# Group norm of a recurrent layer: the heads' mean taken off where the values are turned to rows, and the group norm's products in another order

## The chip, the core and the metric

The kernel runs on one core of one Trainium2 chip. The metric is the device time of one execution in microseconds. PE is the tensor engine (its weight loads are listed apart, as PEld), DVE the vector engine, ACT the scalar engine, POOL the general engine, SP the engine that issues most DMAs. Each has its own queue of instructions, and they meet only at semaphores.

## What is computed

Two transformer blocks in float32, 512 tokens of width 1024. The second block holds an RWKV-7 time mix with 16 heads of 64 channels. The part that the change touches:

```python
o = rwkv7_recurrence(rh, decay, kh, vh, -kk, kk * ah)      # y_t = S_t r_t, S_t += v_t k_t^T, rows of S follow v
o = layer_norm(o, lnx_g.reshape(h, n), lnx_b.reshape(h, n), GN_EPS)   # mean and variance over a head's 64 channels
o = o + jnp.sum(rh * kh * r_k, axis=-1, keepdims=True) * vh           # the bonus
o = o.reshape(bsz, t, wd).astype(p.dtype) * g                         # g = sigmoid(xg) @ g_up
return o @ w_out
```

The recurrence is linear in `v`, channel by channel of a head: the output with the head's mean taken off is the output for values with the head's mean taken off.

## The kernel before

Everything is laid out with channels on the 128 partitions, as 8 blocks of 128 channels (two heads each), and time along the free axis: 528 positions (16 prefix, 512 tokens), of which the last 516 (`T3`, from `O3`) count behind the recurrence. PSUM is `acc[0]` to `acc[3]`, each with two banks; a block of 516 positions is multiplied in two halves of 258, and each half in float32 stands as two PE records. So a multiplication of one block is four PE records.

**`recurrence`** walks over five tiles of time: four of 128 positions and one of 16. In every tile `turn` brings four arrays from channels-by-time to rows-by-channels with `nc.tensor.transpose`, four blocks at a time (`g` is 0 or 1): `TM_V` is the values `v` (the trace's `rw_v`), `TM_A` is `kk` (its `x2r`), `TM_B` and `TM_K` are `a` and `k` (its `rw_a` and `rw_k`). The order on PE is written by hand: `rows_of_v(ti, 0)`, `rows_of_a(ti)`, `rows_of_v(ti, 1)`, then `tail(ti)`, whose first products (`z`, line 2664) need the turned values. ACT copies those from PSUM into `uv` (line 2757), DVE copies part of the others. SP and POOL send small DMAs that invert the diagonal blocks (`at_spill`, `dia`, `inverse`, `MD`, `MTD`).

**`group_norm_and_gate`** is a program block of its own between two barriers, with four hand-written queues. First loop, for each block `i`: PE multiplies `o` by `mean64` (a mean over each head) into `acc[i % 2]`; DVE subtracts it from `o` in place (line 3141); ACT squares the result (line 3114); PE sums squares into 16 rows, one for each head (`of_heads`, line 3064 into `acc[2]`). Beside it DVE makes the product `r * r_k * k` (line 3130), PE sums it over heads by `ones64` into `acc[3]`, and DVE multiplies `v` by it (line 3147). The trace's names: `gn_scratch` is squares and products, `rw_a` is `o`. Then ACT takes the square root over 16 rows (line 3116), DVE the reciprocal (line 3149).

Second loop, for each block `i`: PE spreads the 16 rows to 128 channels (`gn_root` by `gn_own`) into `acc[i % 2]`, DVE multiplies `o` by it (line 3152), ACT applies gain and offset (line 3122), POOL adds the weighted `v` (line 3166), PE makes the gate (`xg` by two slabs of `g_up`, eight records) into `acc[2 + i % 2]`, and DVE multiplies (line 3136). POOL and ACT also split the first two weight slabs of the next stage (`mg_whi`, `mg_wlo`). The next stage, `merge`, begins behind a barrier.

Of the kernel before, what the change touches and what calls it, by code (L numbers as in the profile page):

```python
# [263 lines left out]
def program(nc, x_t, slabs, moe_slabs, params_d, router_bias, const0, const1, const2, meta_rows, final_row, out):  # L264
    top = ExitStack()
    with top:
# [40 lines left out]
        def k0(name, n=P, at=0):  # L307
            return c0[:, C0[name] + at:C0[name] + at + n]
# [2001 lines left out]
        def recurrence(r, k, v, kk, a, o, wc, k2, kk_r, last_y):  # L2310
# [129 lines left out]
            with ExitStack() as nx, block() as b:  # L2440
# [22 lines left out]
                dia, inv = sbt(nx, "dia", [P, 272]), sbt(nx, "inv", [P, 272])  # L2463

# [20 lines left out]
                def _(pe):  # L2485
# [129 lines left out]
                    def turn(ti, w, g, out_bank):  # L2615
                        t0, n = tiles[ti][0:2]
                        for q in range(4):
                            first, count = (t0 + CH, P if stays(ti + 1) else CH) if w == TM_B else (t0, n)
                            mm = nc.tensor.transpose(bank(out_bank)[0:count, q * P:(q + 1) * P],
                                                     arrays[w][:, 4 * g + q, first:first + count], k0("ident"))  # L2620
                        did(mm, "pe", ti, "tm", w, g)
# [21 lines left out]
                    def rows_of_v(ti, g):  # L2643
                        if ti == 0:
                            pe.wait_ge(v_back[0], 16)
                            after(pe, "act", 0, "at", 1)
# [175 lines left out]
                def _(dve):  # L2822
# [84 lines left out]

                    step(nc.vector.memset(S[0][:, :, :], 0.0))
# [133 lines left out]
        def group_norm_and_gate(xt, r, k, v, o, xg, k2, h, w):  # L3042
# [3 lines left out]
            meaned, centred, squared, varred, rooted = (sem("gn_" + n) for n in ("meaned", "centred", "squared", "varred", "rooted"))  # L3046
# [3 lines left out]
            with ExitStack() as nx, block() as b:  # L3050
                view = lambda i: xt[:, 2 * i:2 * i + 2, :].rearrange("p a t -> p (a t)")[:, 0:T3]
                sq, prod = [view(0), view(1)], [view(2), view(3)]
# [5 lines left out]
                owned = sem("gn_owned")  # L3058

                @b.tensor  # L3060
                def _(pe):
                    def over(j, mat, x, rows=P, start=True, stop=True):
                        for s, (lo, hi) in enumerate(halves(T3)):
                            mm = nc.tensor.matmul(acc[j][0:rows, s, 0:hi - lo], mat, x[:, lo:hi], start=start, stop=stop)
                        return mm

                    def variance(i):
                        pe.wait_ge(squared, i + 1)
                        over(2, of_heads(i), sq[i % 2], 16, i == 0, i == 7).then_inc(varred, 1)
# [12 lines left out]
                    n = SLAB0["g_up"]  # L3082
                    pe.wait_ge(sig, 1)
                    slab_wait(pe, n)
                    slab_wait(pe, n + 1)
                    pe.wait_ge(centred, 8)
                    pe.wait_ge(bonus_read, 8)
                    pe.wait_ge(inverted, 1)
                    pe.wait_ge(owned, 1)

                    def gate(i):
                        if i >= 2:
                            pe.wait_ge(gated, i - 1)
                        for q in range(2):
                            mm = over(2 + i % 2, ring[(n + q) % RING][:, i * P:(i + 1) * P], xg[:, q, O3:], P, q == 0, q == 1)
                        mm.then_inc(g_ready, 1)

                    for i in range(8):
# [9 lines left out]
                def _(act):  # L3108
                    nc.scalar.activation(xg[:, :, :], xg[:, :, :], ACT.Sigmoid).then_inc(sig, 1)
                    for i in range(8):  # L3110
# [15 lines left out]
                def _(dve):  # L3126
                    tt = nc.vector.tensor_tensor

                    def product(i):
                        nc.vector.scalar_tensor_tensor(out=prod[i % 2], in0=r[:, i, O3:], scalar=pcol("r_k", i), in1=k[:, i, O3:],  # L3130
                                                       op0=ALU.mult, op1=ALU.mult).then_inc(prod_made, 1)
# [6 lines left out]
                    product(0)  # L3138
                    for i in range(8):
                        dve.wait_ge(meaned, i + 1)  # L3140
                        tt(fold(o[:, i, O3:], T3), fold(o[:, i, O3:], T3), A(i % 2, T3), ALU.subtract).then_inc(centred, 1)
                        if i + 1 < 8:
                            if i >= 1:
                                dve.wait_ge(bonus, i)
                            product(i + 1)
                        dve.wait_ge(bonus, i + 1)
                        tt(fold(v[:, i, O3:], T3), fold(v[:, i, O3:], T3), A(3, T3), ALU.mult).then_inc(bonus_read, 1)
# [11 lines left out]
                def _(pool):  # L3159
                    nc.gpsimd.tensor_copy(own[:, :, :], k0("ident")[0:16, 0:16].unsqueeze(2).to_broadcast([16, 16, 64])).then_inc(owned, 1)  # L3160
                    w.pool(pool, w.ahead("gate_b")[0])
                    for i in range(8):
                        if i == 4:
                            w.pool(pool, w.ahead("gate_b")[1])
# [244 lines left out]
```

## Time and profile before

| | us |
|---|---|
| median of 3 runs | 2117.97 |
| the runs | 2116.71, 2117.97, 2130.38 |
| the profiled execution's own time | 2116.82 |
| its span in the trace | 2115.0 |
| PE busy in the span | 1941.1 (92%) |
| DVE busy | 1305.3 (62%) |
| recurrence, in the trace | about 1280 to 1476 |
| group norm and gate | about 1476 to 1534 |

The profiled execution's time is 1.8 us more than its span, which counts from the first to the last instruction. Its time is 1.15 us under the median. Durations below come from this one execution. In the rows a start and a duration in us stand first; `x4` says that four records were merged; the bracket at the end gives how long the engine had been idle and what ended that.

### The profile page before, as it was taken

How to read it: one execution, taken by the hardware profiler on the slowest of the kernel's cores; microseconds unless marked ns; L12 is line 12 of the kernel's file. 1: busy time of each engine (PE TensorE's matmuls, PEld its weight loads, DVE VectorE, ACT ScalarE, POOL GpSimd, SP SyncE). 2: the span in 40 equal slices, each digit the busy share in tenths (PEclk: the TensorE clock that was granted, in tenths of full speed). 3: DMA queues.
4: the chain of work that ended last, by engine and by line, in shares of the span. 5: the costliest groups of instructions: out<-in, count | busy, mean ns of one | idle time of the engine just before them, and what ended most of it. 6: DMA issues, size and time to landing. Idle time of an engine off the chain costs nothing. (4 is left out here: it accounts for less than half of the span.)

```text
span 2115.0 us, 36683 instructions
## 1 busy us (share of the span) xinstructions
PE 1941.1 (92%) x14678; PEld 1652.9 (78%) x14678; DVE 1305.3 (62%) x2000; ACT 906.9 (43%) x1381; POOL 691.9 (33%) x370
## 2 busy tenths in 40 slices
PE   7999999997999996799999996888999989999997
PEld 4786836764778775799999775787599989999784
DVE  2678758334798997589973674664522178878302
ACT  4314238434788877522233651333242243333312
POOL 2433300330121212243445213320236235555441
PEclk9999999999999998899999898998999999999999
DMA  5222210123999997223223114210042122222221
GB/s 184 90 80 80 80 60 2 61 80 135 401 362 385 360 378 303 70 98 114 91 86 125 61 45 114 36 27 29 20 161 90 51 80 93 90 98 90 78 92 40
DMA packets 91313, 260.08 MB, mean 123 GB/s; under 512 B 26320, under 2 KB 29536, under 8 KB 90528
## 3 DMA queue, kind: packets, MB, share of 16 engines
q1 hardware_dynamic: 87424, 247.90, 32.8%
q0 software_dynamic: 3744, 10.11, 1.4%
q8 instruction: 107, 1.75, 0.3%
q14 instruction: 38, 0.31, 0.0%
HBM read 239.10 MB, written 18.87 MB: 122 GB/s over the span
## 5 line engine op out<-in xcount | busy, mean ns | idle before, releaser
L1578 DVE TENSOR_TENSOR moe_wlo<-moe_ring,moe_whi 128x1024 fp32r<-128x1024 f32 x198 | 233.2, 1224 | 38.8 <-ACT moe_whi L1574 37.8
L547 PE MATMUL acc<-h_xhi,h_whi 128*128 128x264 f32 x816 | 233.5, 286 | 7.0 <-DVE h_xlo L461 3.7
L547 PE MATMUL acc<-h_xlo,h_whi 128*128 128x264 f32 x816 | 233.9, 287 | 0.0
L547 PE MATMUL acc<-h_xhi,h_wlo 128*128 128x264 f32 x816 | 233.5, 286 | 0.0
L1574 ACT ACTIVATE moe_whi<-moe_ring 128x1024 fp32r<-128x1024 f32 x198 | 205.9, 1058 | 40.2 <-PE acc L1635 21.5
L400 POOL TENSOR_TENSOR h_wlo<-ring,h_whi 128x1024 fp32r<-128x1024 f32 x59 | 141.6, 2401 | 249.0 <-ACT h_whi L391 248.8
L547 PE MATMUL acc<-ff_xhi,ff_whi 128*128 128x258 f32 x704 | 200.8, 285 | 9.4 <-DVE ff_xlo L461 9.4
L547 PE MATMUL acc<-ff_xhi,ff_wlo 128*128 128x258 f32 x704 | 199.7, 284 | 0.0
L547 PE MATMUL acc<-ff_xlo,ff_whi 128*128 128x258 f32 x704 | 199.7, 284 | 0.0
L547 PEld LDWEIGHTS acc<-h_xhi,h_whi 128*128 128x128 f32 x816 | 155.8, 191 | 8.6 <-DVE h_xlo L461 4.1
L2141 DVE SCALAR_TENSOR_TENSOR acc<-cp,par,acc 128x528 f32<-128x528 f32 x232 | 159.4, 769 | 0.0
L547 PEld LDWEIGHTS acc<-h_xlo,h_whi 128*128 128x128 f32 x816 | 155.6, 191 | 0.0
L547 PEld LDWEIGHTS acc<-h_xhi,h_wlo 128*128 128x128 f32 x816 | 154.9, 190 | 0.0
L400 POOL TENSOR_TENSOR in_wlo<-ring,in_whi 128x1024 fp32r<-128x1024 f32 x39 | 95.7, 2456 | 156.0 <-ACT in_whi L391 156.0
L400 POOL TENSOR_TENSOR ff_wlo<-ring,ff_whi 128x1024 fp32r<-128x1024 f32 x44 | 115.4, 2626 | 90.4 <-ACT ff_whi L391 90.4
L547 PEld LDWEIGHTS acc<-ff_xhi,ff_whi 128*128 128x128 f32 x704 | 134.1, 190 | 10.9 <-issue 8.3
L547 PEld LDWEIGHTS acc<-ff_xlo,ff_whi 128*128 128x128 f32 x704 | 134.3, 191 | 0.0
L547 PEld LDWEIGHTS acc<-ff_xhi,ff_wlo 128*128 128x128 f32 x704 | 133.8, 190 | 0.0
L547 PE MATMUL acc<-in_xhi,in_whi 128*128 128x512 f32 (+1 forms) x280 | 114.5, 409 | 7.3 <-DVE in_xlo L461 7.3
L3341 DVE SCALAR_TENSOR_TENSOR ff_t<-ff_up,par,ff_t 128x516 f32<-128x516 f32 x44 | 116.2, 2641 | 1.6
L547 PE MATMUL acc<-in_xlo,in_whi 128*128 128x512 f32 (+1 forms) x280 | 111.6, 399 | 0.0
L547 PE MATMUL acc<-in_xhi,in_wlo 128*128 128x512 f32 (+1 forms) x280 | 111.5, 398 | 0.0
(502 smaller groups left out, 4993.9 us busy)
## 6 DMA issues: line engine op xcount, KB each, us to landing
ring<-slabs SPq DMA_DIRECT2D x213, 512.0 KB, 3.5
moe_ring<-moe_slabs SPq DMA_DIRECT2D x204, 512.0 KB, 6.3
tok_rows<-h_tok SPq DMA_DIRECT2D x5, 512.0 KB, 4.0
h_spill<-x2r SPq DMA_DIRECT2D x1, 2112.0 KB, 9.2
v_spill<-rw_v SPq DMA_DIRECT2D x1, 2112.0 KB, 7.4
y_spill<-cp SPq DMA_DIRECT2D x8, 264.0 KB, 4.7
x2r<-h_spill SPq DMA_DIRECT2D x1, 2112.0 KB
x2r<-y_spill SPq DMA_DIRECT2D x1, 2112.0 KB, 10.1
```

Source lines behind the costliest of these rows:

```text
L400: nc.gpsimd.tensor_tensor(self.lo[at][:, :], ring[n % RING][:, :], self.hi[at][:, :].bitcast(F32), ALU.subtract).then_inc(lo_made, 1)
L547: mm = nc.tensor.matmul(acc[j][0:rows, s, 0:t1 - t0], wp[:, at:at + rows], xp[:, t0:t1], start=(k == 0 and m == 0), stop=(k == kt - 1 and ...
L1574: nc.scalar.activation(whi[u % AHEAD][:, :], ringm[u % RAW][:, :], ACT.Copy).then_inc(w_hi, 1)
L1578: tensor_tensor(wlo[u % AHEAD][:, :], ringm[u % RAW][:, :], whi[u % AHEAD][:, :].bitcast(F32), ALU.subtract).then_inc(w_lo[u % 2], 1)
L2141: ins = nc.vector.scalar_tensor_tensor(out=d, in0=x, scalar=tap(q, j), in1=csum(q), op0=ALU.mult, op1=ALU.add)
L3341: nc.vector.scalar_tensor_tensor(out=d, in0=up[i % 4][:, 2:2 + T3], scalar=tap(2), in1=d, op0=ALU.mult, op1=ALU.add).then_inc(tapped, 1)
```

## The change

The recurrence gets a matrix `less_mean` = identity minus the heads' mean (one DVE operation ahead of its first instructions), and `turn` multiplies the values by it instead of transposing them: 40 `transpose` calls become 40 `matmul` calls of the same 128x128 shape (five tiles, two groups, four blocks). The array `v` itself stays, so the bonus still sees the full values. PE waits for the matrix once.

In `group_norm_and_gate` the mean products and DVE's eight subtractions are gone. The products for the bonus are made in place in `r`, so that they need no buffers, and there are four buffers for squares in place of two. ACT squares first and takes the sigmoid after. The bonus products use `acc[0]`, `acc[1]`, `acc[3]` in turn. The first gate stands ahead of the last five bonuses, and in the loop gate `i` now follows spread `i`; before, gate `i - 1` followed it.

```diff
+                less_mean, less_made = sbt(nx, "less_mean", [P, P]), sem("rec_less_mean")
...
-                            mm = nc.tensor.transpose(bank(out_bank)[0:count, q * P:(q + 1) * P],
-                                                     arrays[w][:, 4 * g + q, first:first + count], k0("ident"))
+                            rows, x = bank(out_bank)[0:count, q * P:(q + 1) * P], arrays[w][:, 4 * g + q, first:first + count]
+                            if w == TM_V:
+                                mm = mmul(rows, x, less_mean[:, :], start=True, stop=True)
+                            else:
+                                mm = nc.tensor.transpose(rows, x, k0("ident"))
...
+                    tt(less_mean[:, :], k0("ident"), k0("mean64"), ALU.subtract).then_inc(less_made, 1)
...
PE of group_norm_and_gate:
-                    for i in range(8):
-                        if i >= 2:
-                            pe.wait_ge(centred, i - 1)
-                        over(i % 2, k0("mean64"), o[:, i, O3:]).then_inc(meaned, 1)
-                        pe.wait_ge(prod_made, i + 1)
-                        if i >= 1:
-                            pe.wait_ge(bonus_read, i)
-                        over(3, k0("ones64"), prod[i % 2]).then_inc(bonus, 1)
-                        if i >= 1:
-                            variance(i - 1)
-                    variance(7)
+                    for i in range(8):
+                        pe.wait_ge(squared, i + 1)
+                        over(2, of_heads(i), sq[i % 4], 16, i == 0, i == 7).then_inc(varred, 1)
...
+                    def bonuses(which):
+                        for i in which:
+                            pe.wait_ge(prod_made, i + 1)
+                            if i >= 3:
+                                pe.wait_ge(bonus_read, i - 2)
+                            over(bonus_at(i), k0("ones64"), prod(i)).then_inc(bonus, 1)
...
                     def gate(i):
                         if i >= 2:
                             pe.wait_ge(gated, i - 1)
...
+                    bonuses(range(3))
+                    pe.wait_ge(sig, 1)
...
+                    pe.wait_ge(rooted, 1)
+                    gate(0)
+                    bonuses(range(3, 8))
+                    pe.wait_ge(inverted, 1)
...
                     for i in range(8):
-                        if i >= 2:
+                        if i < 2:
+                            pe.wait_ge(bonus_read, 7 + i)
+                        else:
                             pe.wait_ge(scaled, i - 1)
                         over(i % 2, to_channels(i), root).then_inc(spread, 1)
                         if i >= 1:
-                            gate(i - 1)
-                    gate(7)
+                            gate(i)
ACT:
-                    nc.scalar.activation(xg[:, :, :], xg[:, :, :], ACT.Sigmoid).then_inc(sig, 1)
                     for i in range(8):
-                        act.wait_ge(centred, i + 1)
-                        if i >= 2:
-                            act.wait_ge(varred, i - 1)
-                        nc.scalar.activation(sq[i % 2], o[:, i, O3:], ACT.Square).then_inc(squared, 1)
+                        if i >= 4:
+                            act.wait_ge(varred, i - 3)
+                        nc.scalar.activation(sq[i % 4], o[:, i, O3:], ACT.Square).then_inc(squared, 1)
+                    nc.scalar.activation(xg[:, :, :], xg[:, :, :], ACT.Sigmoid).then_inc(sig, 1)
DVE:
-                    product(0)
                     for i in range(8):
-                        dve.wait_ge(meaned, i + 1)
-                        tt(fold(o[:, i, O3:], T3), fold(o[:, i, O3:], T3), A(i % 2, T3), ALU.subtract).then_inc(centred, 1)
...
+                        nc.vector.scalar_tensor_tensor(out=prod(i), in0=r[:, i, O3:], scalar=pcol("r_k", i), in1=k[:, i, O3:],
+                                                       op0=ALU.mult, op1=ALU.mult).then_inc(prod_made, 1)
+                    weigh(0)
                     dve.wait_ge(rooted, 1)
                     nc.vector.reciprocal(root[:, :], root[:, :]).then_inc(inverted, 1)
+                    for i in range(1, 8):
+                        weigh(i)
```

DVE's second loop is the same as before: for block `i` it multiplies by the spread root, then does the gate product of block `i - 2`. POOL splits both slabs before its additions, and waits in each for `bonus_read` too.

How the instructions stand, first on PE where the second loop begins; `gn_root,gn_own` is a spread, `xg,ring` a gate. Before:

```order
L3064 MATMUL acc2<-gn_scratch,c2 16x258 x4
L3064 MATMUL acc0<-gn_root,gn_own 128x258 x2
L3064 MATMUL acc1<-gn_root,gn_own 128x258 x2
L3064 MATMUL acc2<-xg,ring1 128x258 x2
L3064 MATMUL acc2<-xg,ring2 128x258 x2
L3064 MATMUL acc0<-gn_root,gn_own 128x258 x2
L3064 MATMUL acc3<-xg,ring1 128x258 x2
L3064 MATMUL acc3<-xg,ring2 128x258 x2
L3064 MATMUL acc1<-gn_root,gn_own 128x258 x2
L3064 MATMUL acc2<-xg,ring1 128x258 x2
```

After (bonus products are `x2r,c0`):

```order
L3071 MATMUL acc0<-x2r,c0 128x258 x2
L3071 MATMUL acc1<-x2r,c0 128x258 x2
L3071 MATMUL acc0<-gn_root,gn_own 128x258 x2
L3071 MATMUL acc1<-gn_root,gn_own 128x258 x2
L3071 MATMUL acc3<-xg,ring1 128x258 x2
L3071 MATMUL acc3<-xg,ring2 128x258 x2
L3071 MATMUL acc0<-gn_root,gn_own 128x258 x2
L3071 MATMUL acc2<-xg,ring1 128x258 x2
L3071 MATMUL acc2<-xg,ring2 128x258 x2
L3071 MATMUL acc1<-gn_root,gn_own 128x258 x2
```

The third spread (block 2) was followed by the gate of block 1 in `acc3`; now it is followed by the gate of block 2 in `acc2`, which holds the gate of block 0 until DVE has read it.

On DVE, the start of the group norm (`rw_v,acc` is the bonus put on the values). Before:

```order
L3130 SCALAR_TENSOR_TENSOR gn_scratch<-x2r,par,rw_k 128x516
L3141 TENSOR_TENSOR rw_a<-rw_a,acc0 128x516
L3130 SCALAR_TENSOR_TENSOR gn_scratch<-x2r,par,rw_k 128x516
L3147 TENSOR_TENSOR rw_v<-rw_v,acc3 128x516
L3141 TENSOR_TENSOR rw_a<-rw_a,acc1 128x516
L3130 SCALAR_TENSOR_TENSOR gn_scratch<-x2r,par,rw_k 128x516
```

After:

```order
L3144 SCALAR_TENSOR_TENSOR x2r<-x2r,par,rw_k 128x516 x8
L3136 TENSOR_TENSOR rw_v<-rw_v,acc0 128x516
L3148 RECIPROCAL gn_root<-gn_root 16x516
L3136 TENSOR_TENSOR rw_v<-rw_v,acc1 128x516
L3136 TENSOR_TENSOR rw_v<-rw_v,acc3 128x516
```

All eight products stand first and the subtractions are gone; one bonus multiplication stands ahead of the reciprocal, seven behind it, where all eight were ahead.

## Rows read from the trace of the kernel before

**Rows 1.** Windows of PE: stretch, length, busy, granted clock, DMA share, GB/s.

```profile
1476.00:1502.00 26.00, 25.10 (x96) 0.92 0.22 84
1502.00:1534.50 32.50, 27.70 (x96) 0.84 0.00 1
```

**Rows 2.** Timeline, first vector operation of the group norm, one turn of its first loop.

```profile
1476.47 1.55 DVE L3130 SCALAR_TENSOR_TENSOR gn_scratch<-x2r,par,rw_k 128x516 f32<-128x516 f32 x1 [4.47 <-PEq L2440]
...
1494.79 1.14 PE L3064 MATMUL acc<-rw_a,c 128*128 128x258 f32 x4
...
1495.77 2.01 PE L3064 MATMUL acc<-gn_scratch,c 128*128 128x258 f32 x8
...
1496.69 0.63 ACT L3114 ACTIVATE gn_scratch<-rw_a 128x516 f32<-128x516 f32 x1 [2.28 <-DVE rw_a L3141]
...
1497.71 1.14 PE L3064 MATMUL acc<-rw_a,c 128*128 128x258 f32 x4
```

**Rows 3.** Timeline, from that loop to the spread and gate loop.

```profile
1500.26 1.28 ACT L3116 ACT_TABLE_LOAD   x1
1501.61 0.68 ACT L3116 ACTIVATE gn_root<-acc,c 16x516 f32<-16x516 f32 x1
...
1502.32 3.37 DVE L3149 RECIPROCAL gn_root<-gn_root 16x516 f32<-16x516 f32 x1 [1.87 <-ACT gn_root L3116]
...
1505.93 3.78 PE L3064 MATMUL acc<-gn_root,gn_own 16*128 16x258 f32 x8 [4.37 <-DVE gn_root L3149]
```

**Rows 4.** Timeline, one turn of the spread and gate loop, and its end.

```profile
1519.79 1.14 PE L3064 MATMUL acc<-gn_root,gn_own 16*128 16x258 f32 x4
...
1520.86 2.01 PE L3064 MATMUL acc<-xg,ring 128*128 128x258 f32 x8
1520.97 0.69 DVE L3152 TENSOR_TENSOR rw_a<-rw_a,acc 128x516 f32<-128x516 f32 x1 [1.71 <-PE acc L3064]
1521.58 0.69 DVE L3136 TENSOR_TENSOR rw_a<-rw_a,acc 128x516 f32<-128x516 f32 x1
...
1522.80 1.14 PE L3064 MATMUL acc<-gn_root,gn_own 16*128 16x258 f32 x4
...
1533.74 0.69 DVE L3136 TENSOR_TENSOR rw_a<-rw_a,acc 128x516 f32<-128x516 f32 x1 [1.05 <-PE acc L3064]
...
1536.52 0.36 PE L547 MATMUL acc<-mg_xhi,mg_whi 128*128 128x258 f32 x1 [2.89 <-DVE mg_xlo L461]
```

**Rows 5.** Timeline, the turned values in the fourth of five tiles.

```profile
1435.08 0.66 PE L2619 MATMUL acc<-c,rw_v 128*128 128x128 f32 x4
...
1435.57 1.04 PE L2619 MATMUL acc<-c,x2r 128*128 128x128 f32 x8
1435.77 2.50 ACT L2757 ACTIVATE uv<-acc 64x512 f32<-64x512 f32 x4
...
1436.45 0.60 PE L2619 MATMUL acc<-c,rw_v 128*128 128x128 f32 x4
...
1438.33 1.01 PEld L2664 LDWEIGHTS acc<-uv,M 64*64 64x64 f32 x32 [0.25 <-ACT uv L2757]
```

**Rows 6.** Source line 2702: eight multiplications by the identity.

```profile
L2702 PE MATMUL acc<-c,rw_a x16: 272/272/294, 1280.1 to 1281.7; 128*64 128x128 f32 x16
```

**Rows 7.** Timeline of PE, the wait in the first tile.

```profile
1309.19 3.04 PE L2528 MATMUL acc<-MD,ot 64*64 64x64 f32 x52 [12.64 <-DMA MD<-inverse]
```

**Rows 8.** Windows of PE, as rows 1, for the granted clock.

```profile
1189.50:1204.00 14.50, 14.50 (x52) 0.53 0.16 58
...
1464.00:1466.00 2.00, 2.00 (x22) 0.50 0.00 0
...
1480.00:1482.00 2.00, 1.99 (x9) 0.98 0.97 414
...
1514.00:1516.00 2.00, 2.00 (x9) 0.94 0.00 0
```

**Rows 9.** Groups by line and form, 1180 to 1205.

```profile
L1957 PE MATMUL acc<-late,kk_own 16*128 16x264 f32 x8 | 3.3, 545 | 0.0
```

More of the change, by code:

```diff
@@ L2645, in rows_of_v @@
                             pe.wait_ge(v_back[0], 16)
+                            pe.wait_ge(less_made, 1)
                             after(pe, "act", 0, "at", 1)
@@ L3042, in group_norm_and_gate @@
         def group_norm_and_gate(xt, r, k, v, o, xg, k2, h, w):
-            meaned, centred, squared, varred, rooted = (sem("gn_" + n) for n in ("meaned", "centred", "squared", "varred", "rooted"))
+            squared, varred, rooted = (sem("gn_" + n) for n in ("squared", "varred", "rooted"))
             inverted, spread, scaled, shifted = (sem("gn_" + n) for n in ("inverted", "spread", "scaled", "shifted"))
@@ L3050, in group_norm_and_gate @@
             with ExitStack() as nx, block() as b:
-                view = lambda i: xt[:, 2 * i:2 * i + 2, :].rearrange("p a t -> p (a t)")[:, 0:T3]
-                sq, prod = [view(0), view(1)], [view(2), view(3)]
+                sq = [xt[:, 2 * i:2 * i + 2, :].rearrange("p a t -> p (a t)")[:, 0:T3] for i in range(4)]
+                prod = lambda i: r[:, i, O3:]
                 root = sbt(nx, "gn_root", [16, T3])
@@ L3058, in group_norm_and_gate @@
                 owned = sem("gn_owned")
+                bonus_at = lambda i: (0, 1, 3)[i % 3]
                 @b.tensor
@@ L3096, in gate @@
                         mm.then_inc(g_ready, 1)
+                    bonuses(range(3))
+                    pe.wait_ge(sig, 1)
+                    slab_wait(pe, n)
+                    slab_wait(pe, n + 1)
+                    pe.wait_ge(rooted, 1)
+                    gate(0)
+                    bonuses(range(3, 8))
+                    pe.wait_ge(inverted, 1)
+                    pe.wait_ge(owned, 1)
                     for i in range(8):
-                        if i >= 2:
+                        if i < 2:
+                            pe.wait_ge(bonus_read, 7 + i)
+                        else:
                             pe.wait_ge(scaled, i - 1)
@@ L3108, in _ @@
                 def _(act):
+                    for i in range(8):
+                        if i >= 4:
+                            act.wait_ge(varred, i - 3)
+                        nc.scalar.activation(sq[i % 4], o[:, i, O3:], ACT.Square).then_inc(squared, 1)
                     nc.scalar.activation(xg[:, :, :], xg[:, :, :], ACT.Sigmoid).then_inc(sig, 1)
-                    for i in range(8):
-                        act.wait_ge(centred, i + 1)
-                        if i >= 2:
-                            act.wait_ge(varred, i - 1)
-                        nc.scalar.activation(sq[i % 2], o[:, i, O3:], ACT.Square).then_inc(squared, 1)
                     act.wait_ge(varred, 8)
@@ L3127, in _, with weigh @@
                     tt = nc.vector.tensor_tensor
-                    def product(i):
-                        nc.vector.scalar_tensor_tensor(out=prod[i % 2], in0=r[:, i, O3:], scalar=pcol("r_k", i), in1=k[:, i, O3:],
-                                                       op0=ALU.mult, op1=ALU.mult).then_inc(prod_made, 1)
+                    def weigh(i):
+                        dve.wait_ge(bonus, i + 1)
+                        tt(fold(v[:, i, O3:], T3), fold(v[:, i, O3:], T3), A(bonus_at(i), T3), ALU.mult).then_inc(bonus_read, 1)
                     def gate(i):
@@ L3136, in gate @@
                         tt(fold(o[:, i, O3:], T3), fold(o[:, i, O3:], T3), A(2 + i % 2, T3), ALU.mult).then_inc(gated, 1)
-                    product(0)
                     for i in range(8):
-                        dve.wait_ge(meaned, i + 1)
-                        tt(fold(o[:, i, O3:], T3), fold(o[:, i, O3:], T3), A(i % 2, T3), ALU.subtract).then_inc(centred, 1)
[L3142 to L3147, printed above, removed]
+                        nc.vector.scalar_tensor_tensor(out=prod(i), in0=r[:, i, O3:], scalar=pcol("r_k", i), in1=k[:, i, O3:],
+                                                       op0=ALU.mult, op1=ALU.mult).then_inc(prod_made, 1)
+                    weigh(0)
                     dve.wait_ge(rooted, 1)
                     nc.vector.reciprocal(root[:, :], root[:, :]).then_inc(inverted, 1)
+                    for i in range(1, 8):
+                        weigh(i)
                     for i in range(8):
@@ L3160, in _ @@
                     nc.gpsimd.tensor_copy(own[:, :, :], k0("ident")[0:16, 0:16].unsqueeze(2).to_broadcast([16, 16, 64])).then_inc(owned, 1)
-                    w.pool(pool, w.ahead("gate_b")[0])
+                    for n in w.ahead("gate_b"):
+                        w.pool(pool, n)
                     for i in range(8):
-                        if i == 4:
-                            w.pool(pool, w.ahead("gate_b")[1])
+                        pool.wait_ge(bonus_read, i + 1)
                         pool.wait_ge(shifted, i + 1)
```

9 lines of the change are left out of this document (removed).

## The prediction

> **What bounds the kernel now.** The chain that ended last is of no use here: it reaches back only to the last barrier, far behind this change. So I read the two places one by one in the timeline, each for the wait that ends last, and the granted clock of the tensor engine beside them. In the group norm PE is busy for 25.1 of 26 us in the first loop and 27.7 of 32.5 us in the second [rows 1]. One turn of the first loop lasts from 1494.79 to 1497.71, 2.92 us, for twelve PE records (mean, bonus, variance), while DVE, ACT and POOL have idle time [rows 2]: at full clock a record costs some 0.22 us, and PE is the bound. Between the loops PE stands still for 4.37 us, for the root (0.68) and the reciprocal (3.37) [rows 3]. In the second loop a turn lasts 3.01 us, again twelve records; a spread alone holds PE for 1.07 us (1519.79 to 1520.86), a gate for 1.94 [rows 4]. Both loops so follow PE. The stage lasts from 1476.47 to the end of the last gate product at 1533.74 + 0.69 = 1534.43 [rows 2, 4], 58.0 us. In the recurrence the turned values stand in a chain too: PE turns, ACT copies, and the second half of the `z` products starts when ACT is through [rows 5].
>
> The clock matters at both ends. It is low (0.50 of full, 1.2 of 2.4 GHz) in 1464 to 1466 though PE is busy all of it, at 0.98 in 1480 to 1482, and 0.94 in 1514 to 1516 [rows 8]. From 0.92 over 26 us it was low for 0.08 x 26 x 2 = 4.2 us in the first loop, and from 0.84 over 32.5 us for 10.4 us around the wait for the reciprocal [rows 1].
>
> **The change part by part.** **Turned values.** A transpose is one PE record; in rows 5 eight take 0.88 us (1435.57 to 1436.45), 0.11 each. A float32 multiplication is two records: line 2702, with the same 128 moving columns and weights of 64, has 16 for eight calls, in (1281.7 - 1280.1) / 15 = 0.107 us each [rows 6]. So four calls cost 0.44 us more, and a tile has two groups of four. ACT's copies of the first group start 0.44 later. Those of the second wait for PE: its eight records start 0.44 later than 1436.45 and take 0.88 plus some 0.16 of tail, so ACT starts at 1437.95 and is done two copies (half of 2.50) later, at 1439.2, where `z` now goes on at 1438.33 [rows 5]. That is 0.9 us a tile. Behind it PE has no free time until the next tile's first products, so nothing absorbs it, in four of the five tiles: 3.6 us. In the first tile PE waits 12.64 us for a DMA of the inverse [rows 7], which starts from other data; there it is hidden. Bounds: 0, if other slack takes all, and 4.5 with the first tile. The matrix itself is one DVE operation of 128 elements, ahead of work that DVE waits for anyway: 0 to 0.5 us, taken as 0.
>
> **First part of the group norm.** Gone are 32 mean records and eight subtractions. Squares need nothing now: the first takes 0.63 us [rows 2], and PE starts 0.9 us into the stage. It then has eight variances of four records. At full clock one is 0.87 us; at the low clock 1.72. If the clock rises 3.6 us into the stage, as now, 1.6 variances are done by then and 6.4 x 0.87 = 5.6 follow: 9.2 us. The other rise of this stage came 8.3 us after PE went to work again (1505.93 to 1514.2, from the 0.94) [rows 3, 8]; with that 4.3 variances are low and it is 11.5. I take 10.3. ACT is hidden: eight squares, a table load of 1.28 us [rows 3], a sigmoid over twice the width, so some 1.1 (an estimate), and another load of 1.28 come to 8.7 us, or some 10.2 with the waits for buffers, and the root (0.68) waits for the last variance.
>
> From the end of the variances on: three bonus products on PE, 2.6 us, then the gate of block 0, 1.94. Meanwhile DVE puts the first bonus on the values and starts the reciprocal about 1.8 us behind the variances, done 5.2 us behind them. So 3.37 us of reciprocal now lie beside 4.5 us of PE work, and the 4.37 us gap goes. What is late next is the pair of PE and DVE in bonuses 3 to 7: bonus 4 needs the values of block 1 weighed, and from there each is 0.87 us; the last is weighed 10.4 us behind the variances, and spread 1 starts at 10.5. Spread 0 lies ahead of it. Then 1.07 + 1.94 for spread 1 and gate 1: spread 2 starts at 10.3 + 10.5 + 3.0 = 23.8 us.
>
> **Second loop.** Here the order costs. Gate `i` waits until DVE has read gate `i - 2` from the same bank, and DVE does that behind its product with spread `i`. Before, gate `i - 1` stood there, whose bank was free long ago. A turn is now: spread start to DVE's product 1.18 us (1519.79 to 1520.97), to DVE's gate product 0.61, that product 0.69, some 0.15 back to PE, gate 1.94 [rows 4]: 4.57 us in place of 3.01. Queued behind PE's wait is the next spread, and DVE waits for that. Five turns bring spread 7 to 23.8 + 22.8 = 46.6. Then 2.6 to the start of gate 7, 2.05 until DVE can read it, 0.69: 51.9 us. ACT and POOL, which kept pace with the turn of 3.01, stay hidden in the longer turn. The next stage is reached the same 2.1 us behind DVE's last product as now [rows 4]; its first slabs are freed by the same gate.
>
> **The sum**: 51.9 against 58.0 is 6.1 us less, with ends 7.2 and 4.9 by the clock; with 3.6 more in the recurrence, 2.5 us less. On the profiled execution's 2116.8 that is 2114.3, on the median of 2118.0 it is **2115.5**.
>
> A rule for the turned values: rows 5 and 6 say that a multiplication costs two transposes. The Trainium skill (TensorE: Matmul & The Clock Gate, Terms) says that transpose mode is four times faster for float32. By it a group of four would cost 1.32 us more and not 0.44; it is rival 3 below.
>
> **The rivals.** **1, slower: variances of 16 columns don't raise the clock.** They are 16 columns wide and now stand alone, where they were mixed with full ones. For: in 1464 to 1466 PE is busy all the time with narrow products, at 0.50; from 1189.5 to 1204 it is busy without a gap for 14.5 us at 0.53, in a stage where products of 16 rows, 545 ns each, stand among full ones [rows 8, 9]. Against: those had few rows, these have 128. Then all eight variances take 1.72 us, 13.8 + 0.9 = 14.7, 4.4 more than summed, and the bonuses and the first gate begin low as well, 4.0 more: 8.4 - 2.5 = 5.9 slower, 2123.9. It decides against the change as soon as the clock rises over 2.5 us later than I took.
>
> **2, the clock falls in the second loop.** PE would idle 1.5 of 4.57 us there. For: it fell in the 4.37 us gap before. Against: the gaps are a third of that. Each low turn costs 12 x 0.215 = 2.6 us. A stretch of some 8 us, as now behind the gap, costs 3: 2118.5. The whole loop costs 17: 2132.6.
>
> **3, multiplications at four times a transpose**: 0.88 more a group, eight groups, 7.0 more: 2122.5. Against it stands rows 6, the same form of product.
>
> **4, the second loop doesn't stall**, because the bank is free in time: 6 x 1.56 = 9.4 less, 2106.1. Against it: the order of both queues.
>
> **5, the clock holds in the last tile.** PE ran low from 1464 at the latest until 1480 [rows 8], 12 us of it in the recurrence; if that were at full clock and three quarters of it busy (an estimate), 4.5 less: 2111.0. The Trainium skill (the same page, Part 4: PE-mode transpose) says that transposes don't count as a busy engine. No row here separates that.
>
> **How the numbers follow.** A measurement of this kernel can tell about 1%, 21 us. Chances: my sum 0.50 (its own range 2112 to 2118), rival 1 0.20, rival 2 0.12 for one stretch and 0.04 for the loop, rival 3 0.03, rival 4 0.05, rival 5 0.04, others 0.02. The range reaches from 2109 to 2126: it takes in the sum, rivals 1, 3, 5 and the short form of 2, and leaves out the whole loop, rival 4 and the rest. All of these lie within 1%: 0.97, with 0.01 for faster and 0.02 for slower.
>
> **What the profile would show.** Right: 80 records of `less_mean` with `rw_v`, eight per group 0.107 apart; the tile's `z` 0.9 us later behind its turn; the stage 51 to 53 us; no gap of over 1.5 us on PE around the reciprocal; a turn of 4.5 us in the second loop with PE idle for 1.5 ahead of each gate. Wrong: a granted clock at 0.50 past 8 us of the stage (rival 1) or in the second loop (rival 2); a turn of 3.0 (rival 4). What would upset the sum from outside is a shift of the DMAs of the inverse in the recurrence, which have about 4 us of slack behind PE in the middle tiles.

## The result and the profile after

The changed kernel takes 2130.11 us (median of 20 runs, 2120.04 to 2135.77), the kernel before 2119.45 (20 runs, 2111.84 to 2131.08). The ratio is 1.0039, with a 95% interval of 1.0026 to 1.0053: some 8 us slower (the two medians lie 10.7 apart). That is within 1%, as forecast, but above the range, and on the other side of no change from the 2.5 us less that the sum gave. The profiled execution took 2120.04 us (span 2118.3), the shortest of its 20, so a second one was profiled later (experiment 10).

**The group norm after**, in the timeline: start, duration, work, and in the bracket the idle time before it.

```profile
1478.58 2.20 ACT L3118 ACTIVATE gn_scratch<-rw_a 128x516 f32<-128x516 f32 x4 [0.34 <-PEq L2440]
...
1479.26 9.00 PE L3071 MATMUL acc<-gn_scratch,c 128*16 128x258 f32 x32 [1.35 <-ACT gn_scratch L3118]
...
1489.98 3.36 DVE L3148 RECIPROCAL gn_root<-gn_root 16x516 f32<-16x516 f32 x1
...
1494.04 3.73 PE L3071 MATMUL acc<-x2r,c 128*128 128x258 f32 x16 [0.34 <-DVE rw_v L3136]
...
1501.62 1.13 PE L3071 MATMUL acc<-gn_root,gn_own 16*128 16x258 f32 x4
1504.14 2.01 PE L3071 MATMUL acc<-xg,ring 128*128 128x258 f32 x8 [1.39 <-DVE rw_a L3141]
1506.08 1.14 PE L3071 MATMUL acc<-gn_root,gn_own 16*128 16x258 f32 x4
1508.60 2.01 PE L3071 MATMUL acc<-xg,ring 128*128 128x258 f32 x8 [1.39 <-DVE rw_a L3141]
1510.54 1.14 PE L3071 MATMUL acc<-gn_root,gn_own 16*128 16x258 f32 x4
1513.06 3.14 PE L3071 MATMUL acc<-xg,ring 128*128 128x258 f32 x8 [1.39 <-DVE rw_a L3141]
1516.13 2.08 PE L3071 MATMUL acc<-gn_root,gn_own 16*128 16x258 f32 x4
1519.60 3.81 PE L3071 MATMUL acc<-xg,ring 128*128 128x258 f32 x8 [1.39 <-DVE rw_a L3141]
...
1528.73 2.08 PE L3071 MATMUL acc<-gn_root,gn_own 16*128 16x258 f32 x4
...
1538.89 0.55 PE L547 MATMUL acc<-mg_xhi,mg_whi 128*128 128x258 f32 x1 [2.89 <-DVE mg_xlo L461]
```

Read it against [rows 2 to 4]. The first part is as meant: eight variances in one run of 32 records, done 9.7 us into the stage (1479.26 + 9.00 - 1478.58); the reciprocal lies beside bonuses and a gate, and PE's longest gap there is 0.34 us where it was 4.37. The spread of block 2 starts at 1501.62, 23.0 us into the stage. Then every gate has 1.39 us of idle PE ahead of it, released by DVE's gate product. At first a turn takes 4.46 us. But the same four spread records that last 1.14 us at 1510.54 last 2.08 at 1516.13, and the same eight gate records go from 2.01 to 3.81. The gap has not grown; PE itself has become slow.

**Granted clock**, in windows of PE: stretch, length, busy, granted clock, DMA share, GB/s.

```profile
1478.57:1537.37 58.80, 48.08 (x160) 0.79 0.10 38
1478.57:1503.40 24.83, 23.14 (x92) 0.91 0.23 88
...
1503.40:1513.50 10.10, 6.59 (x26) 1.00 0.00 0
1513.50:1524.00 10.50, 9.12 (x22) 0.51 0.00 0
1524.00:1527.00 3.00, 1.61 (x8) 1.00 0.00 0
1527.00:1537.37 10.37, 7.62 (x18) 0.52 0.03 5
1538.80:1544.80 6.00, 5.91 (x28) 0.52 0.99 376
```

The second loop falls from full clock (1.00, 2.4 GHz) to the lower level (0.51, 1.2 GHz), comes back for 3 us, falls again, and hands the low clock on to the next stage. There, in the kernel before, the clock was up:

```profile
1536.50:1542.50 6.00, 5.98 (x50) 1.00 1.04 414
```

Fifty records there, 28 here in as many microseconds: 22 x 0.12 = 2.6 us lost behind the stage as well. Not all of it comes from the loop: in experiments 1, 2, 3 and 5 to 8, whose loops end at full clock, the same 6 us hold some 37 records, at 0.72. So 9 records, 1.1 us, go with the low clock that the loop hands on. The other 13, 1.6 us, are lost in those seven as well but not in experiment 9, and no run shows why. The whole stage, from the first DMA of the group norm to the first of the next stage, is 58.80 us, and in the kernel before it was 58.57 (1476.43 to 1535.00). In between lies a row of before, the spread of block 2:

```profile
1513.38 1.54 PE L3064 MATMUL acc<-gn_root,gn_own 16*128 16x258 f32 x4
```

It stood 36.9 us into the stage there and stands 23.0 us into it now, 13.9 earlier. From it to the end of DVE's last gate product it was 21.1 us (to 1534.43), and is 35.2 (to 1536.11 + 0.69 = 1536.80), 14.1 more. What the first part gives, the second takes.

**The recurrence after**: the line of the new product, then the fourth tile in PE's timeline, to be held against [rows 5].

```profile
L2622 PE MATMUL acc<-less_mean,rw_v x80: 272/275/583, 1287.5 to 1464.4; 128*128 128x128 f32 x64, 128*16 128x128 f32 x16
```

```profile
1437.14 1.16 PE L2622 MATMUL acc<-less_mean,rw_v 128*128 128x128 f32 x8
1438.13 1.04 PE L2624 MATMUL acc<-c,x2r 128*128 128x128 f32 x8
...
1439.99 1.15 PE L2669 MATMUL acc<-uv,M 64*64 64x64 f32 x32
1441.34 1.15 PE L2669 MATMUL acc<-uv,M 64*64 64x64 f32 x32 [0.20 <-ACT uv L2762]
```

A group of four is eight records and takes 0.99 us (1437.14 to 1438.13), before 0.49. The second half of `z` starts 4.20 us behind the turn, before 3.25 (1435.08 to 1438.33): 0.95 a tile. From the first DMA of the inverse to the group norm it is 176.91 us against 174.74.

### The profile page after: what moved, and what is told of

Same layout as the page of the kernel before. It is cut to its first block and busy times, and to the rows that moved or that the text cites. A ratio compares the mean times of both kernels' runs of the same rounds, so it can differ in the third digit from the quotient of the medians.

```text
span 2118.3 us, 36694 instructions
## 1 busy us (share of the span) xinstructions
PE 1943.8 (92%) x14686; PEld 1656.1 (78%) x14686; DVE 1299.8 (61%) x1993; ACT 906.6 (43%) x1381; POOL 690.6 (33%) x370
## 5 line engine op out<-in xcount | busy, mean ns | idle before, releaser
L547 PEld LDWEIGHTS acc<-ff_xhi,ff_whi 128*128 128x128 f32 x704 | 133.7, 190 | 11.7 <-issue 8.3
```

Source lines behind the costliest of these rows:

```text
L547: mm = nc.tensor.matmul(acc[j][0:rows, s, 0:t1 - t0], wp[:, at:at + rows], xp[:, t0:t1], start=(k == 0 and m == 0), stop=(k == kt - 1 and ...
```

## The experiments

Each ran against the kernel before on the same chip. The ratios have 95% intervals. "Recurrence" below is the stretch from its first `inverse<-inv` DMA to the first DMA of the group norm, "stage" the stretch from there to the first DMA of the next stage, both from the one profiled execution.

**1. The turned values alone**, in the kernel before.

```diff
+                            if w == TM_V:
+                                mm = mmul(rows, x, less_mean[:, :], start=True, stop=True)
+                            else:
+                                mm = nc.tensor.transpose(rows, x, k0("ident"))
```

> The kernel before, with one part of the change alone: the values are turned by the multiplication with less_mean; the group norm is as before, mean products and subtractions too. Theory A (the stall for the gate's bank and the clock it costs explain the slowdown; the turned values cost PE records and no more): the group norm starts 2 to 3.6 us later than before's and lasts 58 us; in all 2 to 4 us slower, ratio 1.001 to 1.002. Theory B (the multiplications disturb the recurrence, by the clock or by the inverse's DMAs, and explain the slowdown): 8 us or more slower, ratio 1.004 or more.

Measured: 2128.44 us, ratio 1.0033 (1.0012 to 1.0055). In its profile the windows of PE give

```profile
1300.69:1482.45 181.76, 148.44 (x3872) 0.88 0.15 27
1482.45:1540.72 58.27, 52.49 (x192) 0.88 0.11 39
```

The stage is that of before, the recurrence 7 us longer. Its fourth tile reads as in the changed kernel (`z` 4.21 us behind the turn), so the records explain four times 0.95 us. The rest goes with the granted clock, 0.88 over this stretch where it was 0.90, and is seen in places: the 26 us from 1344 to 1370 ran at 1.00 in the kernel before and at 0.87 here and in the changed kernel, while 1396 to 1404 went from 0.79 to 1.00. The turned values alone are a loss. Their 1.0033 lies between the two expectations, and its interval holds both: it allows the 3.6 us summed, and it allows all of the changed kernel's loss. It takes the next experiment to tell the theories apart.

**2. The gate one block behind the spread again**, all else as changed.

```diff
                         over(i % 2, to_channels(i), root).then_inc(spread, 1)
-                        if i >= 1:
-                            gate(i)
+                        if i >= 2:
+                            gate(i - 1)
+                    gate(7)
```

> The changed kernel with one order undone: in the second loop gate i-1 follows spread i again, for i from 2, and gate 7 comes last; gate 0 stays early. Theory A: a turn falls from 4.46 to 3.0 us, PE idles under 0.5 us in it, the clock stays at full, and the stage lasts 58.2 - 5 x 1.45 - 5 or so for the clock = 46 to 49 us; in all 8 to 14 us faster than the changed kernel, so 0.995 to 0.999 of before. Theory B: the stage gets shorter, but the total stays within 3 us of the changed kernel's, since the loss sits in the recurrence. Theory C (the clock falls in this loop whatever the order, from 16-row products): the turn is 3.0 us at full clock but low-clock turns of over 5 us stay.

Measured: 2109.93 us, 0.9942 (0.9921 to 0.9963). Timeline of PE in the second loop:

```profile
1503.68 3.08 PE L3071 MATMUL acc<-gn_root,gn_own 16*128 16x258 f32 x12
1506.69 3.60 PE L3071 MATMUL acc<-xg,ring 128*128 128x258 f32 x8
1510.22 1.14 PE L3071 MATMUL acc<-gn_root,gn_own 16*128 16x258 f32 x4
1511.29 2.01 PE L3071 MATMUL acc<-xg,ring 128*128 128x258 f32 x8
1513.23 1.14 PE L3071 MATMUL acc<-gn_root,gn_own 16*128 16x258 f32 x4
```

```profile
1484.02:1528.44 44.42, 42.01 (x160) 0.90 0.14 51
1506.70:1509.90 3.20, 3.20 (x9) 0.50 0.01 3
```

No bracket, so no idle time, and turns of 3.01 us as in [rows 4]. The gain is more than was expected (46 to 49 us of stage, a ratio of 0.995 at best): moving one call takes 14.4 us off the stage and turns a loss of 0.4% into a gain of 0.6%. The order of the second loop is the cause; whether by the wait itself or by the clock that follows from it is the next question.

One thing here is not explained by waits. The clock is low for 3.2 us from 1506.70 on, with PE busy all the time and 0.34 us its only gap since the variances began. In this order three spreads stand in a row ahead of that stretch, twelve records of 16 rows. Experiments 5, 7 and 8 have the same loop, and each has its low stretch at that place (9.7 us long in experiment 5); experiment 6, with two spreads in a row and a single gap of 0.19 us, has none. That the narrow products bring it fits, but no run here varies them alone.

**3. The changed kernel with PE kept busy in the wait**: three products by the identity into columns of the other product's bank that nobody uses.

```diff
                         if i >= 2:
+                            for f in range(3 if i < 7 else 0):
+                                nc.tensor.matmul(acc[3 - i % 2][:, f % 2, 258:512], k0("ident"), xg[:, 0, O3:O3 + 254], start=True, stop=True)
                             pe.wait_ge(gated, i - 1)
```

> The changed kernel with work added in the wait: ahead of PE's wait for the gate's bank, in turns 2 to 6 of the second loop, three useless 128x128 products over 254 columns (six records, 1.3 us at full clock) go to unused columns of a bank that nobody reads then. The stall of 1.39 us stays in time but PE is busy in it. Theory A split in two: if the clock falls because PE idles, the granted clock stays at 1.00 to the end of the loop, the turn stays at 4.5 us, and the stage lasts 51 to 53 us in place of 58.2, 5 to 8 us faster than the changed kernel. If the clock falls for another reason, low turns get longer than 7.2 us and the kernel is slower than the changed one.

Measured: 2123.13 us, 0.9997 (0.9979 to 1.0015).

```profile
1516.17 1.14 PE L3071 MATMUL acc<-gn_root,gn_own 16*128 16x258 f32 x4
1517.24 1.55 PE L3090 MATMUL acc<-xg,c 128*128 128x254 f32 x6
1518.69 2.01 PE L3071 MATMUL acc<-xg,ring 128*128 128x258 f32 x8
1520.63 1.14 PE L3071 MATMUL acc<-gn_root,gn_own 16*128 16x258 f32 x4
```

```profile
1492.33:1544.39 52.06, 48.27 (x190) 0.94 0.12 44
1545.90:1551.90 6.00, 5.99 (x37) 0.72 1.01 370
```

All turns take 4.46 us, and none is low, though the gap ahead of gate 7 is left open. The wait is as long as before; only PE is busy in five of its six turns. The order and the spreads are the same, so in this loop it is the gaps that bring the clock down. That the spreads' 16 rows have no part in it isn't shown: the filling products have 128 rows, and experiment 2 had a low stretch without a gap. This is the kernel that the prediction described: its last gate product ends 51.5 us into the stage (DVE's line at 1543.12 and its 0.69), beside the 51.9 of the sum. Against experiment 2 it prices the wait at 7.6 us of stage (11.7 by the ratios, but each has an interval of some 4 us to either side), and against the changed kernel the clock at 6.7 us of stage in this profile, and 1.0039 - 0.9997 = 0.42%, 9 us, in the times.

**4. The kernel before with the gate at once**, nothing else changed.

```diff
                         over(i % 2, to_channels(i), root).then_inc(spread, 1)
-                        if i >= 1:
-                            gate(i - 1)
-                    gate(7)
+                        gate(i)
```

> The kernel before, with the gate's place alone changed: gate i follows spread i for all i, and waits for gate i-2 to be read. Everything else is as before. Theory A: turns of 4.46 us and more from turn 2 on, PE idle 1.39 us in each, clock down in part of the loop; the stage lasts 64 to 72 us, 6 to 14 us slower than before, ratio 1.003 to 1.007. Theory B: within 3 us of before.

Measured: 2139.46 us, 1.0095 (1.0065 to 1.0125), the slowest of all, and slower than was expected (6 to 14 us more, a stage of 64 to 72).

```profile
1520.94 2.08 PE L3064 MATMUL acc<-gn_root,gn_own 16*128 16x258 f32 x4
1524.41 3.81 PE L3064 MATMUL acc<-xg,ring 128*128 128x258 f32 x8 [1.39 <-DVE rw_a L3134]
1528.14 2.08 PE L3064 MATMUL acc<-gn_root,gn_own 16*128 16x258 f32 x4
```

```profile
1477.49:1556.59 79.10, 65.02 (x192) 0.72 0.08 28
```

The same gap of 1.39 us, and turns of 7.20 us: here the clock has just come back from the gap for the reciprocal (a turn of 3.01 us, from 1512.77), and it falls in the first turn that has a gap. The stage grows by 20.5 us and the time by 0.95%, 20 us. Of the 4.2 us more per turn the wait is 1.45 (4.46 less 3.01) and the clock 2.74 (7.20 less 4.46).

**5. Experiment 2 with the values turned by a transpose.**

```diff
-                            if w == TM_V:
+                            if False:
                                 mm = mmul(rows, x, less_mean[:, :], start=True, stop=True)
```

> The kernel with gate i-1 behind spread i (the second experiment's), with the values turned by plain transposes again. It leaves out that the heads' mean is taken off, so its output is that without the mean removed; every other instruction stays. Theory A (a multiplication costs its extra PE records, 0.9 us a tile on the path, and at times a stretch of low clock): 4 to 7 us faster than the second experiment's kernel, 0.991 of before; from the first inverse's DMA to the start of the group norm 175 to 177 us in place of 183. Theory D (the turn is hidden, and the first experiment's 0.33% had another reason): the same time as the second experiment's kernel within 2 us.

This kernel leaves out that the heads' mean is taken off, so it is a yardstick and no choice.

Measured: 2104.42 us, 0.9922 (0.9893 to 0.9951), with a profiled execution of 2122.24, the slowest of its six. Beside experiment 2 (0.9942) it is 0.20%, 4 us, less, but the intervals overlap. The profiles agree better: the recurrence with transposes took 174.74, 177.09, 174.75 and 177.51 us (before, experiments 4, 9 and this one), mean 176.0; turned by the matrix in the changed order, 176.91, 181.76, 183.14, 182.14, 179.72 and 181.22 (changed, 1, 2, 3, 6, 10), mean 180.8. That is 4.8 us for five tiles, with one profile of each kernel and a spread of 6 us among the second six.

**6. DVE's gate product first**: in the changed kernel DVE does the gate of block `i - 2` before it waits for spread `i`.

```diff
                     for i in range(8):
-                        dve.wait_ge(spread, i + 1)
-                        tt(fold(o[:, i, O3:], T3), fold(o[:, i, O3:], T3), A(i % 2, T3), ALU.mult).then_inc(scaled, 1)
                         if i >= 2:
                             gate(i - 2)
+                        dve.wait_ge(spread, i + 1)
+                        tt(fold(o[:, i, O3:], T3), fold(o[:, i, O3:], T3), A(i % 2, T3), ALU.mult).then_inc(scaled, 1)
```

> The changed kernel with PE's order left as changed and DVE's order altered: in turn i of the second loop DVE does the gate product of block i-2 ahead of its product with spread i. If the slowdown is PE's wait for the bank that DVE reads too late (theory A), the wait goes: a turn is 3.0 us, PE idles under 0.5 us, the clock stays up, and the stage lasts about 44 us as in the second experiment, 0.994 of before. If it is that the gate of the same block stands directly behind its spread on PE, whatever DVE does (rival), turns stay at 4.4 us and more and the total stays near the changed kernel's.

Measured: 2109.7 us, 0.9956 (0.994 to 0.9972).

```profile
1508.50 1.14 PE L3071 MATMUL acc<-gn_root,gn_own 16*128 16x258 f32 x4
...
1509.57 2.01 PE L3071 MATMUL acc<-xg,ring 128*128 128x258 f32 x8
```

PE keeps the changed order and hardly waits (0.19 us once, ahead of gate 2): the spread at 1508.50 and the next at 1511.51 are 3.01 us apart, the granted clock is 1.00 through the loop, and the stage is 44.03 us. So the loss lies in the pair of orders, and either side mends it.

**7. Both groups of values turned first**, with the loop of experiment 2: in each tile, so that ACT's copies of the second group don't follow the turn of `kk`.

```diff
                             rows_of_v(ti, 0)
-                            rows_of_a(ti)
                             rows_of_v(ti, 1)
+                            rows_of_a(ti)
```

> The second experiment's kernel, with the turn of the values ahead in each tile: both groups of values, then kk, where kk stood between the two groups. If what is on the path is ACT's copies behind PE's second group (theory A), the z products' second half goes on 3.3 to 3.8 us behind the turn's start in place of 4.2, and the kernel is 1 to 3 us faster than the second experiment's. If PE's records alone are the path (rival), the total is the same within 1 us, since as many records stand there.

Measured: 2107.38 us, 0.9936 (0.9917 to 0.9956).

```profile
1438.71 2.05 PE L2622 MATMUL acc<-less_mean,rw_v 128*128 128x128 f32 x16
...
1441.57 2.08 PE L2669 MATMUL acc<-uv,M 64*64 64x64 f32 x64
```

`z` now runs in one piece and its second half starts about 3.9 us behind the turn (1438.71 to 1441.57 and half of 2.08), 0.3 less, where 0.4 to 0.9 less was expected. The recurrence is 179.81 us. Its gain over experiment 2 can't be told from none, so which of the two theories holds stays open. It has the lowest ratio of the kernels here that compute everything: 0.6% faster than the kernel before.

**8. Every turned value multiplied twice**, with the loop of experiment 2, to get a price with a larger lever.

```diff
                             if w == TM_V:
+                                mmul(rows, x, less_mean[:, :], start=True, stop=True)
                                 mm = mmul(rows, x, less_mean[:, :], start=True, stop=True)
```

> The second experiment's kernel with the suspected cost doubled: each multiplication that turns values is issued twice to the same place, so 160 records of 0.11 us where there were 80. Theory A: two groups of 0.88 more in four tiles, 7.0 us more on the path, so 7 to 10 us slower than the second experiment's kernel (0.998 of before). Theory D (the turn is hidden): under 3 us slower.

Measured: 2115.44 us, 0.998 (0.9961 to 0.9999); recurrence 190.45 us.

```profile
1298.72:1489.17 190.45, 155.94 (x3936) 0.88 0.14 26
```

The trace has 64 more records in this stretch than experiment 2 (3936 against 3872), 64 x 0.11 = 7.0 us of PE, and the recurrence is 7.3 us longer (183.14 there); by the ratios it is 0.38%, 8 us. So the records on this path are paid for, and no slack swallows them. The agreement to 0.3 us is partly luck: against the mean of 180.8 above, the stretch is 9.6 us longer. The change itself has 32 more in this stretch (3872 against 3840 before), 3.5 us by the same price; the sum had 3.6, and the profiles give 4.8.

**9. The kernel before with PE kept busy while it waits for the reciprocal**: nine products by the identity into `acc[1]`.

```diff
                     pe.wait_ge(bonus_read, 8)
+                    for f in range(9):
+                        nc.tensor.matmul(acc[1][:, f % 2, 258:512], k0("ident"), xg[:, 0, O3:O3 + 254], start=True, stop=True)
                     pe.wait_ge(inverted, 1)
```

> The kernel before, with work added in the wait between its two loops: while DVE takes the reciprocal, PE does nine useless 128x128 products over 254 columns (18 records, 3.8 us at full clock) into unused columns of a bank that nobody reads then. The wait of 4.37 us stays. If the low clock behind that wait comes from PE standing still (theory A), the second loop starts at full clock, its first turns take 3.0 us in place of 5, and the stage lasts 54 to 55 us in place of 58; 3 to 5 us faster than before, 0.998. If the clock falls there for another reason, the stage stays at 58 and the total at 1.000.

Measured: 2113.55 us, 0.9974 (0.9951 to 0.9997).

```profile
1498.26 4.12 PE L3089 MATMUL acc<-xg,c 128*128 128x254 f32 x18
1502.50 2.01 PE L3064 MATMUL acc<-gn_root,gn_own 16*128 16x258 f32 x8
```

```profile
1473.24:1527.60 54.36, 52.83 (x210) 0.97 0.11 42
```

The first two spreads take 2.01 us where they took 3.78 [rows 3], and the stage is 4.2 us shorter with 18 records of useless work in it. The low clock behind that gap cost 4.2 us, about as much as the gap of 4.37.

**10. The changed kernel again**, for a second profile.

> The changed kernel once more, for a second trace of it: the first, at 2120.0 us, was the fastest of its 20 executions (median 2130.1). Theory A expects of a slower execution that the second loop has more turns at low clock than the first trace, up to all six, at 7.2 us each, and the stage lasts up to 70 us; the recurrence takes 177 to 183 us from the first inverse's DMA to the group norm. If the slower executions lose their time elsewhere, the stage is 58 us as in the first trace.

Measured: 2130.84 us, 1.0035 (1.0011 to 1.0059).

```profile
1509.62 1.14 PE L3071 MATMUL acc<-gn_root,gn_own 16*128 16x258 f32 x4
1512.14 3.42 PE L3071 MATMUL acc<-xg,ring 128*128 128x258 f32 x8 [1.39 <-DVE rw_a L3141]
```

```profile
1485.58:1549.34 63.76, 53.02 (x160) 0.71 0.10 35
```

The clock falls in the first gated turn, where in the other profile it held for two, and the loop goes on low: turns of 5.87, 5.39, 7.21, 7.20 and 7.21 us, a stage of 63.8. One and the same program gives 58.8 or 63.8 us here, with identical gaps. The first profile of the changed kernel, the fastest of its 20 runs, had understated the loss. But this execution took 15.1 us longer than that one, and the stage has only 5.0 of them: 4.3 lie in the recurrence, 2.7 ahead of it and 3.1 behind the stage.

## Why the prediction was wrong

**Right.** The turned values: 80 records, 0.99 us for eight where 0.88 was taken, hidden in the first tile (PE still waits 11.15 us there for `MD`), `z` 0.95 us late in the fourth, where 0.9 was forecast. The first part of the group norm: variances done at 9.7 us (10.3 forecast), the spread of block 2 at 23.0 (23.8). The wait of the second loop: 1.39 us of idle PE in turns of 4.46 (1.5 in 4.57). With the clock held up (experiment 3) the last gate product ends 51.5 us into the stage, by the sum 51.9, and the ratio of 0.9997 has the 2.5 us less of the sum in its interval. Each mechanism but the clock was there at about its forecast size, and the sum of them was the sum of another kernel.

**The step that failed** is the one on the clock in the second loop: rival 2 was put aside with "the gaps are a third of that", that is, gaps of 1.5 us were taken to be mostly harmless because they are shorter than the one of 4.37, behind which the clock had been low. Experiments 3 and 10 show otherwise: with the gaps filled every turn stays at 4.46 us, with them open turns reach 7.21. Filling them gives back 9 us of the 10.8 by which the change missed its forecast (8.3 more in place of 2.5 less). The end of the last gate product at 1536.80 is 58.2 us into the stage, 6.3 more than the sum: 4.3 in the five turns (27.1 in place of 22.8), 2.7 from spread 7 on (8.1 in place of 5.3), 0.8 less ahead of them. To it come 2.6 us in the next stage, 1.1 of them from the low clock that the loop hands on; the sum had no term for it and ended with the stage. In experiment 10 the stage takes 5 us more still.

**Rival 2** was thus the case that came about, with 0.16 in its two forms, and its two sizes hold the measured ones between them: 3 us for a stretch and 17 for the loop, where the two profiles of the stage show 6.7 and 11.7 beyond experiment 3. The range left the longer form out. A row that should have raised its chance stood in the prediction: 0.50 from 1464 to 1466 with PE busy all of it [rows 8]. A clock that is low without a long gap just there should not have been priced by the length of one gap.

Two slips in the clock's terms did not decide anything. With a rise 8.3 us after PE's start, and that start 0.9 us into the stage, the slow bound of the variances is 12.0 us and not 11.5. And a later rise costs only half of its delay (0.87 us a variance against 1.72), so it would take some 5 us more, not 2.5, to turn the forecast gain into a loss.

**The turned values** were summed at 3.6 us, and cost 4.8 in the mean of the profiles (7 in experiment 1, with 3.6 inside its interval). The records are priced right; that some is added by other stretches at low clock, such as 1344 to 1370, is seen in the windows, but no experiment here shows why they lie where they do.

**Rival 1** fell: the clock came up inside the stretch of variances, so 16 columns did not keep it down. Two windows of the changed kernel:

```profile
1482.50:1483.00 0.50, 0.50 (x2) 0.50 1.13 473
...
1483.50:1486.00 2.50, 2.50 (x13) 1.00 0.69 290
```

That is some 4.5 us into the stage, where 3.6 had been seen before. **Rival 3** fell with the 80 records: a group of four costs 0.50 us more than its transposes, not 1.32: here a multiplication costs two transposes. The Trainium skill (TensorE: Matmul & The Clock Gate, Terms) has transpose mode four times faster for float32; this trace shows a factor of two, and the measurement decides. **Rival 4** did not come about, but experiments 2 and 6, which make it true, show its price somewhat high: 6 x 1.56 = 9.4 us of sum, 7.6 to 8.0 us of stage against experiment 3. **Rival 5** came about in small part at most: the clock was low in the last tile again, but for less of it. The last 16 us of the recurrence ran at 0.71 in the changed kernel and 0.58 before; over all profiles it is 0.66 to 0.74 with the values multiplied and 0.58 to 0.62 with them transposed (before, experiments 4, 5 and 9). What that is worth was not measured apart.

## What to carry to other kernels

Where a loop is bound by one engine with a granted clock, price a new wait in it twice: the wait itself, and all of that engine's work around it at the lower clock, into the stage behind. When a double-buffered product is moved nearer to its consumer's turn, write down for both queues which reader frees its bank, and in what position: here one call one block too early on PE, or one operation one place too late on DVE, cost more than all that the rest of the change saved. Measure such a change in parts: the turned values alone are a loss, but they are the price for taking the mean products out of the group norm, and together with the old order of the second loop they are a gain of 0.6%. Only the new place of the gate paid for nothing.

## What the runs showed of the hardware that was not expected

- With gaps of 1.39 us in turns of 4.46 us the granted clock went from 1.00 to 0.50, in one profile from the first such turn on, in another behind two of them; experiment 4 had three turns of 7.2 us in a row. With short useless products in the gaps it stayed at 1.00. The Trainium skill (TensorE: Matmul & The Clock Gate, A second HAM failure mode: psum-queue depth-cycling) tells of another kernel whose engine idles briefly and often between groups of products while it cycles through PSUM banks, and whose clock swings for it; these traces agree, with the numbers above.
- A low stretch came without a gap, too: behind three spreads in a row (twelve records of 16 rows) the granted clock was 0.50 for 3.2 us in experiment 2 and for 9.7 in experiment 5, with PE busy all the time. What brings it was not tested.
- Work added can make a stage shorter: 18 records of it in the gap for the reciprocal took 4.2 us off the stage and 0.26% off the time.
- At the same gaps, the time lost to the clock differs from one execution of a program to the next (stages of 58.8 and 63.8 us). One profile of such a loop gives a sample of its cost, no measurement.
